# Own buffers and other places for the constants of the spatial gate in a decoder layer on Trainium2

## What is computed

```python
h = x @ w_in + b_in                       # -> q | k | v | z (= u, v) | gate_a | gate_g
y_a = sliding_window_attention(q, k, v, sinks) @ w_br_a      # window 128
# chunked spatial gating on gelu(z), chunks of 128 positions, 8 groups of 128 channels:
v = layer_norm(v, ln_g, ln_b)
w = jnp.where(causal[None], w_s, 0.0)                        # (8, 128, 128)
mixed = jnp.einsum('gts,bnsgd->bntgd', w, vc) + b_s.T[None, None, :, :, None]
y_g = (u * mixed) @ w_br_g
mix = sigmoid(gate_a) * y_a + sigmoid(gate_g) * y_g
x = layer_norm(alpha * x + mix @ w_out)
x = layer_norm(alpha * x + squared_relu_mlp(x, w_up, w_down))
```

## Time and profile before

| | us |
|---|---|
| median of 3 executions | 1069.91 (1069.44 to 1070.71) |
| the profiled execution's own time | 1070.79 |
| span of its slowest core (core 6) | 1069.2 |
| spans of the eight cores | 1067.0 to 1069.2 |
| mean granted clock of TensorE | 0.983 to 0.988 |
| TensorE busy in the span | 1010.6 (95%) |

### The profile page before, as it was taken

How to read it: one execution, slowest core, us unless ns; L and a number is a source line. 1 busy time by engine, 2 the same in 40 slices (tenths; PEclk the granted TensorE clock), 3 DMA queues, 4 the chain that set the end, 5 groups by cost and what they waited for, 6 DMA issues and landing times.

```text
span 1069.2 us, 16775 instructions; the slowest of 8 cores (1067.0 to 1069.2 us)
## 1 busy us (share of the span) xinstructions
PE 1010.6 (95%) x5892; PEld 495.2 (46%) x6002; DVE 597.2 (56%) x1062; ACT 375.7 (35%) x502; POOL 94.9 (9%) x152
## 2 busy tenths in 40 slices
PE   4975999999999999999999999999999999999995
PEld 1432645555444444444444565555544444444442
DVE  0707647776678521233788545777566842124377
ACT  0251467674142410132003457777314341013200
POOL 4101000000021000000122100000001100000011
PEclk9996999999999999999999999999999999999998
DMA  9992424323369770594149632422437366068012
GB/s 155 184 183 60 80 40 66 55 41 100 60 142 155 153 131 1 79 158 79 60 101 205 120 68 40 80 41 41 99 80 137 66 133 118 1 97 141 1 60 99
DMA packets 19090, 99.17 MB, mean 93 GB/s; under 512 B 2368, under 2 KB 3008, under 8 KB 10048
## 3 DMA queue, kind: packets, MB, share of 16 engines
q0 software_dynamic: 11808, 73.41, 41.9%
q1 hardware_dynamic: 7200, 24.68, 6.7%
HBM read 163.09 MB, written 8.39 MB: 160 GB/s over the span
## 4 chain that ended last, share of the span: by engine, by line
PE 87%; DMA 7%; DVE 2%; issue 2%; ACT 1%; POOL 0%; DVEq 0%; POOLq 0%; another core or an unknown queue 0%; ACTq 0%; SPq 0%
PE ps L409 57%; PE ps L1073 20%; PE ps L850 3%; DMA ring<-wst 2%; DMA reg<-trilT 2%; PE ps L815 2%; DMA reg<-ident 2%; PE ps L868 2%; PE ps L724 1%; DMA reg<-wsT 1%; PE ps L898 1%; PE ps L989 1%; PE ps L671 1%; ACT scr L392 1%; PE ps L612 0%
## 5 line engine op out<-in xcount | busy, mean ns | idle before, releaser
L409 PE MATMUL ps<-reg,ring 128*128 128x512 bf16 x1495 | 339.7, 379 | 2.6 <-issue 0.6
L409 PE MATMUL ps<-xT_s,ring 128*128 128x512 bf16 (+1 forms) x1081 | 248.4, 376 | 4.6 <-DMA xT_s<-xh 1.5
L392 ACT ACTIVATE scr<-ps 128x512 f32<-128x512 f32 (+1 forms) x192 | 141.2, 737 | 284.9 <-PE ps L409 252.0
L409 PEld LDWEIGHTS ps<-reg,ring 128*128 128x128 bf16 x1536 | 147.2, 98 | 173.4 <-issue 3.0
L1073 PE MATMUL ps<-ring,reg 128*128 128x512 bf16 x1004 | 220.6, 379 | 1.1
L409 PEld LDWEIGHTS ps<-xT_s,ring 128*128 128x128 bf16 x1120 | 104.7, 98 | 118.5 <-issue 8.2
L1073 PEld LDWEIGHTS ps<-ring,reg 128*128 128x128 bf16 x1024 | 100.2, 98 | 120.8
L381 DVE SCALAR_TENSOR_TENSOR reg<-ps,scr 128x512 bf16<-128x512 f32 x128 | 87.7, 691 | 113.1 <-ACT scr L392 113.0
L823 DVE CUSTOM_DVE_ANT_1 scr<-ps,masks 128x1024 f32<-128x1024 f32 x64 | 78.1, 1220 | 59.8 <-PE ps L815 36.2
L434 POOL DMA_DIRECT2D ring<-wst x64 | 35.8, 586 | 490.1 <-PE ps L409 182.5
L392 ACT ACTIVATE scr<-scr,amx 128x1024 bf16<-128x1024 f32 x64 | 73.2, 1144 | 14.6 <-DVE amx L381 10.9
(11 more groups left out here) (64 smaller groups left out, 618.4 us busy)
## 6 DMA issues: line engine op xcount, KB each, us to landing
ring<-wst POOLq DMA_DIRECT2D x64, 1024.0 KB, 10.9
regK<-x SPq DMA_DIRECT2D x16, 512.0 KB, 6.1
y<-scr SPq DMA_DIRECT2D x15, 512.0 KB, 2.6
lnbuf<-lnrep SPq DMA_DIRECT2D x4, 1024.0 KB, 20.4
xT_s<-xt POOLq DMA_DIRECT2D x2, 1024.0 KB, 21.7
xT_s<-xt POOLq DMA_DIRECT2D x7, 256.0 KB, 26.5
ring<-wst POOLq DMA_DIRECT2D x7, 256.0 KB, 21.0
regK<-bzv SPq DMA_DIRECT2D x2, 512.0 KB, 12.6
```

Source lines behind the costliest of these rows:

```text
L392: return timed(P.op("act", lambda e: e.activation(out=out, in_=in_, func=func, bias=bias, scale=scale), reads=R, writes=W), 0.28 + width(o ...
L409: r = e.matmul(out, lhsT=a, rhs=b, start=(k == 0), stop=(k == 7))
```

## The change

The three blocks get buffers of their own (`B_cst` stays with t01, `B_tri` for t2 and `B_idf` for idf). `load_consts` now holds tril, wsT, ident and bs, in this order, and is called two stages sooner, after the first pair of k tiles of half 1 of blocks 0 to 3; only its first load, tril, carries the condition. The other four loads make `load_more_consts`, called where `load_consts` was, and only its first load, brow, carries the condition. `prepare_consts` moves from ahead of the norm of block 4 to behind the statistics of block 5, `spatial_bias` behind those of block 6. The sinks are prepared at q.

```diff
+        B_tri, B_idf = Buf("tri"), Buf("idf")
+
         def load_consts(after):
-            ld(t01, wsT_d.rearrange("p g t -> p (g t)"), [B_cst], after)
-            ld(t2, trilT_d[:, :], [B_cst])
-            ld(idf, ident_d[:, :], [B_cst])
+            ld(t2, trilT_d[:, :], [B_tri], after)
+            ld(t01, wsT_d.rearrange("p g t -> p (g t)"), [B_cst])
+            ld(idf, ident_d[:, :], [B_idf])
             ld(Cg[:].rearrange("p g t -> p (g t)"), bs_d[:, :], [C["Cg"]])
-            ld(brow[:], brow_d[:, :], [C["brow"]])
+
+        def load_more_consts(after):
+            ld(brow[:], brow_d[:, :], [C["brow"]], after)
             ld(masks[:, 0, :], amask_d[:, :], [C["masks"]])
+            ld(sinks[:], sinks_d[:, :], [C["sinks"]])
             ld(masks[:, 1, :], amask0_d[:, :], [C["masks"]])
-            ld(sinks[:], sinks_d[:, :], [C["sinks"]])
 
         def prepare_consts():
             tt(wsTb[:], t01.rearrange("p (g t) -> p g t", g=8), t2.unsqueeze(1).broadcast_to([128, 8, 128]), ALU.mult,
-               [B_cst], [C["wsTb"]])
-            cp(identb[:], idf, [B_cst], [C["ident"]])
+               [B_cst, B_tri], [C["wsTb"]])
+            cp(identb[:], idf, [B_idf], [C["ident"]])
...
                     ALU.mult, ALU.add, [B_ps[b + gi // 4], C["bcol"], C["Cg"]], [C["Cg"]])
+
+        def prepare_sinks():
             ts(negsink[:], sinks[:], -1.0, ALU.mult, [C["sinks"]], [C["sinks"]])
...
                 zv_half(0, 0, range(3, 4), True)
-                zv_half(0, 1, range(4), True)
+                load_consts([zv_half(0, 1, range(1), False)])
+                zv_half(0, 1, range(1, 4), True)
...
                 o = zv_half(1, 0, range(1), False)
-                load_consts([o])
+                load_more_consts([o])
...
-                rest = [prepare_consts, lambda: [zv_B(4), spatial_bias()], lambda: [zv_B(5), zv_C(4)], lambda: [zv_B(6), zv_C(5)],
+                rest = [lambda: zv_B(4), lambda: [zv_B(5), zv_C(4), prepare_consts()], lambda: [zv_B(6), zv_C(5), spatial_bias()],
                         lambda: [zv_B(7), zv_C(6)], lambda: zv_C(7)]
...
-                Prog.alias_after(B_at, [B_cst, C["ones"]])
+                Prog.alias_after(B_at, [B_cst, B_tri, B_idf, C["ones"]])
...
+            if prev is None:
+                prepare_sinks()
             for e_ in range(8):
                 q_unit(e_, 0)
```

## The result

The changed kernel takes 1055.01 us (median of 4, 1054.65 to 1057.23) against 1069.91 for the kernel before in the same comparison: a ratio of 0.9864, 95% interval 0.9845 to 0.9883, so 14.9 us faster where 17.4 were forecast. Measured again, unaltered, with the last experiments, it takes 1055.61 us, ratio 0.9856 (0.9841 to 0.9871). Both lie in the range of 1048 to 1060. One of the four executions of the kernel before fell in a slower state of the chip (1264.78 us), and all medians and ratios here are of executions outside it.

The account below looks back on a forecast made before the run. TensorE, busy 1010.6 of 1069.2 us, was held 18.2 us by ident, last of three chained loads. The terms -18.2 - 2.3 + 3.1 = -17.4 us took the median from 1069.91 to 1052.5 us, range 1048 to 1060.

Parts of the forecast that it names:

- Step 1: Own buffers for tril and ident: TensorE's 18.2 us wait for identb goes, and 2.3 us of low clock behind it.
- Step 2: Sinks prepared at q: VectorE's 24.3 us standstill goes and norms come sooner; counted as nothing, since TensorE's z_u covers it.
- Step 3: wsT, ident and bs, unconditioned, are issued from about 2.4 us and delay the first weights: +3.1 us, bounds 0 and 7.6.
- Step 4: bzv lands behind wsT, ident and bs at 32.9 us, before its 35.0 limit: no stall; other end 8.3 us.
- Step 5: TensorE's wait for xh, the halo, stays about 1.4 us though lnbuf passes before: zero, bounds 1.5 less, 3 more.
- Step 6: VectorE's new waits for wsTb and Cg at the spatial gate don't hold TensorE: zero, up to 5 us.
- (b): Rival: the start pays more for the early loads than counted; chance 0.16.
- (a): Rival: the early issue costs nothing, as SP's loads fit in gaps of POOL's queue: 1049.4 us; chance 0.10.
- (d): Rival: slower, bzv lands so late (67.2 us) that blocks 4 to 7 stand still: 1084.7 us; chance 0.04.
- (e): Rival: the change doesn't do what it says; the identb wait stays and only changes its releaser; chance 0.01.
- (c): Rival: VectorE becomes the bound at the spatial gate, TensorE waiting up to 5 us: 1057.5 us; chance 0.17.

Follow-up runs that it names:

- e2: Kernel before with own buffers for tril and ident, old condition on the constants, sinks still prepared in the spatial bias: 1067.48 us, ratio 0.9972.
- e4: Kernel before with only the sinks prepared at q: 1069.73 us, ratio 0.9994.
- e1: Changed kernel with the condition on wsT, ident and bs as well as tril, so none is issued ahead of bzv: 1050.11 us, ratio 0.9811.
- e9: Changed kernel with all constants behind the old late condition, in order of use, and lnbuf held until the last v product: 1048.87 us, ratio 0.9791.
- e10: Changed kernel with the condition on wsT too, so ident and bs pass in front: 1053.08 us, ratio 0.9832.
- e11: Changed kernel with the condition on ident too, so wsT and bs pass in front: 1052.84 us, ratio 0.9827.
- e7: Changed kernel with the condition on wsT and ident too, so only bs passes in front: 1051.20 us, ratio 0.9810.
- e3: Kernel before with own buffers for tril and ident and sinks prepared at q, without the earlier issue: 1053.70 us, ratio 0.9844.

## Why the prediction was right, and where its terms were off

**Step 1** (own buffers, -18.2 and -2.3 of clock): right. The wait is gone, and the clock is 1.00 from 71 to 93 us. Between the two marks 23.0 us went where 20.5 were counted. Of the 2.5 more, 1.5 are the wait for xh on core 6, 1.0 to 2.5 on the seven cores whose rows show it.

**Step 2** (sinks at q, nothing by itself): right in both directions, which e2 and e4 show. Without it own buffers are worth 3 us (part of what e2 lacks is its wait for bs), and it alone is worth none.

**Step 3** (where the loads really go, +3.1): the mechanism is right to the place. wsT is issued at 2.44, ident and bs behind it, lnbuf right behind tril at 33.86. The size is the term that failed. Undoing the early issue gives 4.9 us (e1), and from no load in front (e9) to the changed kernel the first z_u matmul moves by 5.2 and 5.8 us in the mean of the two profiles. Against the kernel before it moved by 5.9, of which 3.8 are idle time and 2.0 are slow matmuls, about 630 ns instead of 380. The 3.1 priced the idle time, and was 0.7 short there. The speed of TensorE at the start had no term at all, though step 1 counts the clock behind its standstill. In the two profiles, up to the first mark and over the eight cores, each of the ten idle gaps of TensorE over 3 us has 5 to 8 slow matmuls among the next eight, and 46 of the 55 gaps of 0.3 to 2 us have none; six of the ten are in the changed kernel. That is the larger part of what was missing.

The share of ident was mis-sized too. I had 1.4 for wsT and 0.3 for ident, and the runs show 1 to 2 us for either (e10, e11). So ident, "nearer to nothing, by size", was priced by the wrong quantity; its 128 packets of 512 bytes, where wsT has 128 of 4096, fit what it cost better than its 64 KB. And bs, for which I had another 1.4, shows no cost when it is alone (e7). I also left out amask, the sinks, tril and lnbuf, though I had placed them between bzv and the first z_u weights; six cores wait 0.8 to 2.3 us for those weights. Amask and the sinks go beside the first weights in the changed kernel, right behind bzv.

The packet rate itself, on the core whose rows the prediction used (DMA queues of core 6, changed kernel, 13 to 20 us):

```profile
q0 software_dynamic: 393, 0.72, 70.2%
q1 hardware_dynamic: 244, 0.66, 32.8%
```

Against 554 packets, 161 of POOL's gave way to 244 of SP's, 0.66 for one, where the earlier trace rows had 0.88. Over all eight cores in the same stretch POOL's queue lost 132 packets of 561 in the mean to 254 more of SP's, 0.52 for one, and a single core passes anything from 504 to 616 before the change. So the price of a packet was not too low. With amask and the sinks there are 640 packets instead of 384, 128 for each load, and 640 x 0.52 / 80 is 4.2 us, near to the 3.8 of idle time. But that sum is argued: no run moved those two loads alone. What e7, e10 and e11 leave for them is little. The steps add up to 48.7 + 1.2 + 2.2 = 52.1 without them, and the changed kernel has 52.6 and 52.0 with them; by the means of the spans 1049.7 without them stands against 1050.5 and 1051.2, so 0.8 to 1.5 us are left, where 256 packets at that price are 1.7.

**The metric is the slowest core.** The mean of the eight spans fell from 1068.3 to 1051.0, by 17.3, which is the forecast of 17.4 almost to the digit. That is luck: the two errors, 2.5 too little gained and 2.8 too little lost, cancel. The measured time fell by 14.9, because the start is now uneven: the latest of eight cores is 3.2 us behind the mean, where it was 1.5, and the slowest span is 2.9 to 4.7 us over the mean of its execution, where it was about 1.7. The prediction worked with one core's rows and had no term for the spread.

**Step 4** (bzv behind the others): the first use is at 32.98 on core 7 where 33 was forecast, but that core is the latest. On core 6, whose rows the forecast used, it is at 27.97, and on the eight cores at 26.7 to 33.0; on four of them bzv has landed before TensorE is ready for it. So the rate of 26 packets a us fits core 7 and was too low for core 6, and that the number is met is in part chance. As forecast, no core waits for a bank at the first matmuls of blocks 4 to 7. Two cores wait 1.1 to 1.2 us on VectorE (L387) before the first z_u matmul, which may be its remainder; it wasn't tried. **Step 5** (xh): the wait I left standing is gone. The planner put the halo's products behind spatial products, at 87.94 on core 7, when xh has landed (63.6 us after its issue at 11.44). I had assumed the order of before. The lnbuf that passes before it is 128 packets of 8192 bytes in both profiles, where I counted 256. **Step 6** (new waits on VectorE): right, `wsTb` waits for no load on any core, and `Cg` for TensorE only, 3.0 to 3.4 us. The same step done without an earlier issue (e3) does wait, TensorE 3.2 to 5.3 us behind `Cg`, for bs, which I had not listed among the loads that can be late.

**The rivals.** (b), that the start pays more, is what happened beside the forecast: 5.9 us where 3.1 were counted. Packets did not cost more for that: POOL's queue lost 0.5 to 0.7 for each of SP's, fewer than the 0.88 of the earlier trace rows. The rest is 0.7 us of further idle time and 2.0 us of slow matmuls, and for the slowest core the spread between cores. (a), (d) and (e) are out. (c) is out for this kernel; e3 has a wait at that place, made by a load and not by VectorE's work.

## What to carry to other kernels

If a planner or a compiler may reorder loads, a condition on the first load of a group holds only that one. Look where the others are really issued, for a load with no condition goes to the front of the queue and is paid for by the transfers that the first matmuls wait for. The loads here had an earliest time, when they stopped being in the way, and a latest, set by their place in the queue (bs, fourth in e3, landed 31 us after its issue): 1 MB at 2 us cost 5 us, the same at 37 us in the wrong order made TensorE wait 3 to 5 us elsewhere, and at 37 us in the order of use it made it wait for nothing. Longer waits for weights cost twice here, 3.8 us as idle time and 2.0 as slow matmuls; price both. And when an engine's standstill is hidden behind another one, remove both together: here each by itself gave 2.8 us (e2) and nothing that can be told apart (e4, ratio 0.9994), and the two together 16.6 (e3).

## What the runs showed of the hardware that was not expected

A load of 64 KB in 128 rows delayed the start by about as much as one of 512 KB in 128 rows: by the first z_u matmul 1.2 and 2.2 us, by TensorE's idle time 1.8 and 1.8, by the mean span 0.9 and 1.2. Beside POOL's full queue (its share of the 16 engines was 96 to 107% from 13 to 20 us before the change) the cost of a load did not shrink with its bytes where its packets stayed as many. SP's own issue of a load, 0.33 us for bzv and for tril, took 1.53 us for ident at 3.10 us and up to 1.95 us for the sinks in the changed kernel. And the eight cores, with the same program and no exchange between them, reach the same matmul 3.6 us apart before and 5.7 after the change. With two or three of the loads in front the spread is 5.1 to 6.6 us, in the kernels with one or none 2.6 to 4.3; but lnbuf late makes it 4.7, and lnbuf in front as well makes it 4.8 and not more.
